# Low-rank gate of a two-layer decoder step: unrounded 32-bit products in quarters of the array in place of split products over its whole width

## The reference

```python
h = rms_norm(x, norm_g)                     # 2048 wide
proj = h @ w_in                             # c_lr is 16 of its columns
log_a = jax.nn.log_sigmoid((c_lr @ w_gate_lr + b_gate).astype(jnp.float32)) / C_GATE_TAU
o_c, new_S = gla_chunked(gq, gk, gv, log_a.reshape(bsz, L, C_HEADS, C_DK), gla_state)
```

## Time and profile before

| | us |
|---|---|
| median of three runs | 2256.7 |
| the profiled execution's own time | 2256.36 |
| its span, first to last instruction | 2254.6 |
| TensorE busy in it | 2247.4 (100% of the span) |
| VectorE busy | 1376.5 (61%) |
| ScalarE busy | 982.7 (44%) |

### The profile page before, as it was taken

The page is one execution under the profiler, slowest core; times in us unless marked ns, Lnnn a source line. Parts: engine busy times, 40 slices in busy tenths (PEclk is TensorE's granted clock), DMA queues, the critical chain, the costliest instruction groups (busy, mean ns, idle before and its releaser), DMA issues.

```text
span 2254.6 us, 40415 instructions
## 1 busy us (share of the span) xinstructions
PE 2247.4 (100%) x16664; PEld 2224.5 (99%) x16664; DVE 1376.5 (61%) x2453; ACT 982.7 (44%) x1788; POOL 77.6 (3%) x122
## 2 busy tenths in 40 slices
PE   9999999999999999999999999999999999999999
PEld 9999999999999999999999999999999999999999
DVE  6777767765545545446657777677645545545443
ACT  6454355644333333333344543556443333333332
POOL 1100100000000000000011001000000000000000
PEclk9999999999999999999999999999999999999999
DMA  7443654334444444445563437543344444444454
GB/s 287 150 160 132 233 195 141 129 126 150 150 150 150 150 150 150 150 150 196 191 220 134 161 129 247 192 149 112 130 149 151 150 150 150 151 150 151 149 197 150
DMA packets 100071, 364.12 MB, mean 162 GB/s; under 512 B 12288, under 2 KB 13056, under 8 KB 99056
## 3 DMA queue, kind: packets, MB, share of 16 engines
q1 hardware_dynamic: 88896, 317.76, 42.0%
q0 software_dynamic: 10128, 42.43, 5.3%
q10 hardware_dynamic: 864, 1.36, 0.2%
HBM read 341.65 MB, written 20.50 MB: 161 GB/s over the span
## 4 chain that ended last, share of the span: by engine, by line
PE 95%; DVE 2%; ACT 1%; issue 1%; DMA 0%; ACTq 0%; DVEq 0%
PE main L1693 90%; PE side L1693 4%; PE side L1697 1%; DVE w_lo L514 1%; ACT w_hi L1212 0%; DMA x_first<-in_x_pairs 0%; DVE sums L529 0%; PE side L1910 0%; PE side L1834 0%; DVE lev_e L778 0%; DVE ta L533 0%; PE side L1917 0%; DVE lev_q L529 0%; DVE lev_k L785 0%; DVE ext L600 0%
## 5 line engine op out<-in xcount | busy, mean ns | idle before, releaser
L514 DVE TENSOR_TENSOR w_lo<-raw,w_hi 128x512 fp32r<-128x512 f32 x1184 | 784.7, 697 | 493.4 <-ACT w_hi L1212 488.3
L1693 PE MATMUL main<-xg_hi,w_hi 128*128 128x320 f32 x3488 | 1084.4, 311 | 1.5 <-DVE w_lo L514 1.4
L1693 PE MATMUL main<-xg_lo,w_hi 128*128 128x320 f32 x3488 | 1077.2, 309 | 0.0
L1693 PE MATMUL main<-xg_hi,w_lo 128*128 128x320 f32 x3456 | 1067.9, 309 | 0.0
L1212 ACT ACTIVATE w_hi<-raw 128x512 fp32r<-128x512 f32 x1184 | 709.3, 626 | 695.2 <-PE main L1693 671.6
L1693 PEld LDWEIGHTS main<-xg_hi,w_hi 128*128 128x128 f32 x3488 | 654.8, 188 | 5.4 <-DVE xg_lo L548 1.5
L1693 PEld LDWEIGHTS main<-xg_lo,w_hi 128*128 128x128 f32 x3488 | 655.0, 188 | 0.2
L1693 PEld LDWEIGHTS main<-xg_hi,w_lo 128*128 128x128 f32 x3456 | 648.8, 188 | 0.0
L1693 PE MATMUL main<-branch_hi,w_hi 128*128 128x320 f32 x768 | 237.3, 309 | 0.0
L1693 PE MATMUL main<-branch_lo,w_hi 128*128 128x320 f32 x768 | 237.3, 309 | 0.0
L1693 PE MATMUL main<-branch_hi,w_lo 128*128 128x320 f32 x768 | 237.3, 309 | 0.0
(11 more groups left out here) (253 smaller groups left out, 1292.3 us busy)
## 6 DMA issues: line engine op xcount, KB each, us to landing
raw<-in_w_stream SPq DMA_DIRECT2D x595, 512.0 KB, 3.3
state<-in_state POOLq DMA_DIRECT2D x16, 512.0 KB, 4.8
out_state_s<-state POOLq DMA_DIRECT2D x16, 512.0 KB, 3.9
turned<-normed SPq DMA_DIRECT2D x40, 80.0 KB, 2.1
w_pool<-in_w_pool POOLq DMA_DIRECT2D x2, 1024.0 KB, 7.4
cache_k<-in_cache_k POOLq DMA_DIRECT2D x2, 1024.0 KB, 5.0
cache_v<-in_cache_v POOLq DMA_DIRECT2D x2, 1024.0 KB, 8.0
out_k_window<-in_cache_k_tok POOLq DMA_DIRECT2D x2, 960.0 KB, 10.3
```

The lines of the kernel that those rows point to most:

```text
L514: dve.tensor_tensor(w_lo[Q % RAWS][:, half], raw[Q % RAWS][:, half], w_hi[Q % HIS][:, half].bitcast(F32), ALU.subtract).then_inc(lo_ready, 1)
L1693: return pe.matmul(out, lhsT, rhs, start=start, stop=stop)
```

## The change

The blocks of the two low-rank beats are no longer rounded and split. DVE multiplies their 16 useful columns for each piece with the normalization gain into `w_rank` (`scale_rank`, one instruction for each of the two blocks). TensorE multiplies this with the plain x (`x_first`) as 32-bit floats, in four column quarters of the array: quarter q holds the 16 columns at 32 q and takes tokens 80 q to 80 q + 79. In layer 1 `x_first` is filled again from `y_mid` by eight loads of 320 KB, for which TensorE waits. The result lies in four row quarters; DVE reads it in four instructions of 16 x 80. The gate products run in four row quarters, 16 products of 16 rows with 128 columns and 80 tokens. The gate weights come in four loads for each layer, not eight. Since the two blocks need no `w_hi` buffer, the splits of blocks 10, 11 and 12 are put one or two beats earlier in the programs of ACT and DVE (`split_ahead`).

```diff
+def split_ahead(Q):
+    at = {LR_AT - 2: LR_AT + 2, LR_AT - 1: LR_AT + 2, LR_AT: LR_AT + 3, LR_AT + 1: LR_AT + 4}
+    return Q - Q % BEATS + at.get(Q % BEATS, Q % BEATS + 2)
...
+            def scale_rank(Q):
+                l, part = Q // BEATS, Q % BEATS - LR_AT
+                dve.wait_ge(raw_in[Q % RAWS], 16 * (Q // RAWS) + 16)
+                gain = par[:, l, R_NG + 8 * part:R_NG + 8 * part + 8].unsqueeze(2).to_broadcast([P, 8, RANK])
+                dve.tensor_tensor(w_rank[:, part, :].rearrange("p (k c) -> p k c", k=8),
+                                  raw[Q % RAWS][:, :].rearrange("p (k c) -> p k c", k=8)[:, :, 0:RANK], gain,
+                                  ALU.mult).then_inc(rank_ready, 1)
...
-                    dve.tensor_tensor(ta[:, 0, :], group_psum(GROUPS * l + LR_GROUP)[:, 0, :], rstd[:, :],
-                                      ALU.mult).then_inc(main_free, 1)
+                    low = group_psum(GROUPS * l + LR_GROUP)
+                    for q in range(4):
+                        rows, cols = slice(32 * q, 32 * q + RANK), slice(QUARTER * q, QUARTER * q + QUARTER)
+                        last = dve.tensor_tensor(ta[rows, 0, 0:QUARTER], low[rows, 0, 0:QUARTER], rstd[rows, cols],
+                                                 ALU.mult)
...
-                    split_lo_to(Q + 2)
+                    split_lo_to(split_ahead(Q))
...
-                    split_hi_to(Q + 2)
+                    split_hi_to(split_ahead(Q))
...
+                    for j in range(PAIRS):
+                        load(x_first[:, 2 * j:2 * j + 2, :], ins["y_mid"][j], x_again_in)
...
+            def rank_products(l, part, G):
+                bank = 2 * (G % 2)
+                pe.wait_ge(rank_ready, LR_BEATS * l + part + 1)
+                if l:
+                    pe.wait_ge(x_again_in, 16 * PAIRS)
+                for kk in range(8):
+                    k = 8 * part + kk
+                    for q in range(4):
+                        last = mm(main[32 * q:32 * q + RANK, bank, 0:QUARTER], w_rank[:, part, RANK * kk:RANK * kk + RANK],
+                                  x_first[:, k, QUARTER * q:QUARTER * q + QUARTER], k == 0, k == KT_D - 1)
+                    if kk % 4 == 3:
+                        last.then_inc(half_used, 1)
...
-                        rows = slice(2 * RANK * h, 2 * RANK * h + 2 * RANK)
-                        last = mm(side[:, h, 0:TOK], w_gate[rows, :], ta[rows, 0, :])
+                        for q in range(4):
+                            rows = slice(32 * q, 32 * q + RANK)
+                            last = mm(side[:, q, QUARTER * h:QUARTER * h + QUARTER], w_gate[rows, DK * h:DK * h + DK],
+                                      ta[rows, 0, 0:QUARTER])
```

More of the change, by code:

```diff
@@ L76, with is_rank, split_no, split_block @@
 LR_GROUP = LR_AT // 4
+QUARTER = TOK // 4
+def is_rank(Q):
+    return LR_AT <= Q % BEATS < LR_AT + LR_BEATS
+def split_no(Q):
+    l, beat = divmod(Q, BEATS)
+    return Q - LR_BEATS * (l + (beat >= LR_AT + LR_BEATS))
+def split_block(n):
+    l, i = divmod(n, BEATS - LR_BEATS)
+    return BEATS * l + i + (LR_BEATS if i >= LR_AT else 0)
+def split_ahead(Q):
+    at = {LR_AT - 2: LR_AT + 2, LR_AT - 1: LR_AT + 2, LR_AT: LR_AT + 3, LR_AT + 1: LR_AT + 4}
+    return Q - Q % BEATS + at.get(Q % BEATS, Q % BEATS + 2)
 C_COS, C_SIN, C_IDENT, C_BLOCK, C_KEEP, C_INVC, C_BSEL, C_END = 0, 320, 640, 768, 896, 1216, 1280, 1288
@@ L338, in trunk @@
         ones_r = place("ones_r", [P, P], F32R)
-        w_gate = place("w_gate", [P, DK], at=part_c + 12288 + 6144)
+        w_rank = place("w_rank", [P, LR_BEATS, 8 * RANK])
+        w_gate = place("w_gate", [P, GH * DK], at=part_c + 12288 + 6144)
         sq_hi = place("sq_hi", [P, 2, TOK], F32R, at=part_c + 8 * T1)
@@ L363, in trunk @@
         hi_ready = sem("hi_ready")
+        rank_ready = sem("rank_ready")
+        x_again_in = sem("x_again_in")
         lo_ready = sem("lo_ready")
@@ L469, in exchange @@
                             normed[32 * (q ^ 1):32 * (q ^ 1) + 32, :, :]).then_inc(swapped, 16)
[L471 to L479, removed]
         block = ctx.enter_context(nc.Block())
@@ L500, in split_lo_to @@
                 while lo_next[0] <= min(Q, BEATS * DEPTH - 1):
-                    split_lo(lo_next[0])
+                    (scale_rank if is_rank(lo_next[0]) else split_lo)(lo_next[0])
                     lo_next[0] += 1
@@ L507, in split_lo @@
                     half = slice(512 * s, 512 * s + 512)
[L508 to L513, removed]
-                    dve.tensor_tensor(w_lo[Q % RAWS][:, half], raw[Q % RAWS][:, half],
-                                      w_hi[Q % HIS][:, half].bitcast(F32), ALU.subtract).then_inc(lo_ready, 1)
+                    dve.wait_ge(hi_ready, split_no(Q) * 2 + (s + 1))
+                    dve.tensor_tensor(w_lo[Q % RAWS][:, half], raw[Q % RAWS][:, half],
+                                      w_hi[split_no(Q) % HIS][:, half].bitcast(F32), ALU.subtract).then_inc(lo_ready, 1)
+            def scale_rank(Q):
[5 more added lines that the diff above has]
+                                  ALU.mult).then_inc(rank_ready, 1)
             def wait_step(l, name, k):
@@ L679, in log_decay @@
                 for h in range(GH):
-                    v(dve.tensor_scalar(lev_q[:, h, :], side[:, h, 0:TOK], col(l, R_BG + h), None, ALU.add))
+                    v(dve.tensor_scalar(lev_q[:, h, :].rearrange("p (q t) -> p q t", q=4),
+                                        side[:, :, QUARTER * h:QUARTER * h + QUARTER], col(l, R_BG + h), None, ALU.add))
                 v.settle()
@@ L992, in vector_part @@
                     dve.wait_ge(half_used, last_half(l, beat))
-                    dve.tensor_tensor(ta[:, 0, :], group_psum(GROUPS * l + LR_GROUP)[:, 0, :], rstd[:, :],
-                                      ALU.mult).then_inc(main_free, 1)
+                    low = group_psum(GROUPS * l + LR_GROUP)
[3 more added lines that the diff above has]
+                                                 ALU.mult)
+                        if q < 3:
+                            v(last)
+                    last.then_inc(main_free, 1)
                     marks[("lr", l, 0)] = (main_free, GROUPS * l + LR_GROUP + 1)
@@ L1195, in split_hi_to @@
                 while hi_next[0] <= min(Q, BEATS * DEPTH - 1):
-                    split_hi(hi_next[0])
+                    if not is_rank(hi_next[0]):
+                        split_hi(hi_next[0])
                     hi_next[0] += 1
@@ L1206, in split_hi @@
                     if Q >= HIS:
[L1208 to L1212, removed]
+                        act.wait_ge(half_used, 2 * split_block(split_no(Q) - HIS) + s + 1)
+                    act.activation(w_hi[split_no(Q) % HIS][:, half], raw[Q % RAWS][:, half], ACT.Copy).then_inc(hi_ready, 1)
             def wait_step(l, name, k):
@@ L1548, in load_gate @@
             def load_gate(l):
[L1550 to L1553, removed]
+                for q in range(4):
+                    load(w_gate[32 * q:32 * q + RANK, :], ins["w_gate"][l], w_gate_in)
             load_gate(0)
@@ L1714, in block_products @@
                 for s in range(2):
-                    wh, wl = w_hi[Q % HIS], w_lo[Q % RAWS]
+                    wh, wl = w_hi[split_no(Q) % HIS], w_lo[Q % RAWS]
                     if opening is not None:
                         wait_mark(pe, "xg", opening, k0 // 2 + s)
-                    pe.wait_ge(lo_ready, Q * 2 + (s + 1))
+                    pe.wait_ge(lo_ready, split_no(Q) * 2 + (s + 1))
                     pairs = [(kk, t) for kk in range(2) for t in range(tiles)]
@@ L1740, in side_step @@
                     wm("rms_taken", l, 0)
-                    pe.wait_ge(w_gate_in, 128 * l + 128)
+                    pe.wait_ge(w_gate_in, 64 * l + 64)
                     for h in range(GH):
-                        rows = slice(2 * RANK * h, 2 * RANK * h + 2 * RANK)
-                        last = mm(side[:, h, 0:TOK], w_gate[rows, :], ta[rows, 0, :])
+                        for q in range(4):
+                            rows = slice(32 * q, 32 * q + RANK)
+                            last = mm(side[:, q, QUARTER * h:QUARTER * h + QUARTER], w_gate[rows, DK * h:DK * h + DK],
+                                      ta[rows, 0, 0:QUARTER])
                 elif name == "level":
@@ L1935, in _ @@
                             wait_main(G, G - 1)
-                        rank_products(Q, G, 8 * part, part == 0, part == 1)
+                        rank_products(l, part, G)
                     else:
```

## The result

The changed kernel takes 2262.68 us (median of ten runs, 2261.96 to 2266.23) against 2256.68 us before (ten runs, 2255.87 to 2258.55): ratio 1.0028, 95% interval 1.0020 to 1.0036. It is slower by 6.0 us. The forecast was 2258.6 us with a range up to 2262.0, so the prediction is wrong. What happened lies between its forecast and its third rival: block 10 landed later than forecast, but not as late as the rival had it, and a fall of the clock, which no rival had, came on top.

A forecast was written before the change was run, and what follows sets the result against it. Two tied chains, TensorE's and the gate's, were taken to bound the kernel and absorb the saving: 2256.36 + 0.5 (layer 0) + 1.7 (layer 1) = 2258.6 us, range 2254.3 to 2262.0.

The forecast's parts named there:

- third rival: Layer 1: window copies hold block 10 for 11.5 us, or x lands as late; +5.1, time 2262.0; chance 0.14.
- The low-rank products: Low-rank beats, each layer: 32 rounds of 70 ns, 2.57 us with switching against 4.70 before; TensorE saves 2.1 us.
- the 24 ns for each 16-column product: Low-rank products: 40 products in 0.96 us, taken to show the 60-cycle overhead is shared by quarters; 1.6 us left out.
- The gate products: Gate step, each layer: 1.25 us with switching against 0.95 before, 0.3 us slower (0 to 0.4).
- Layer 0: Layer 0: TensorE stands 0.7 us for cq, masks and lev_q start later, block 13 ready 0.5 us later: +0.5 us.
- the sign that was named: Layer 0: lev_q at 47.5 to 48.2 us, listed among the signs of a right prediction.
- Layer 1, the landing of block 10: Layer 1: block 10, issued at 1151.89, taken to land at 1160.0, nearest to block 9's row; +1.7 us.
- the prediction's own formula: Layer 1: loss is block 10's landing less 1158.3; time is 2256.36 + 0.5 + 1.7 = 2258.6 us.
- The clock: Layer 1: no clock term; after a 3.6 us stand, products 2.48, beat 10 3.52, gate step 1.25.
- x itself: Layer 1: x's loads, ahead of the copies, land about 1156 us; needed at 1159.3.
- The rule on the queues: Layer 1: no packet rule is written out; the third rival has the window copies hold block 10 11.5 us, chance 0.14.

The follow-up runs named there:

- late copies and the order near the old one: Changed kernel with the window copies moved into the mixing beats and only block 8 split ahead of cq at beat 6: 2253.82 us, ratio 0.9990.
- late masks: Changed kernel with window copies in the mixing beats, only block 8 split ahead of cq, and layer 0's masks at beat 16, not 10: 2253.14 us.
- the smaller pieces: Changed kernel with each window copy issued as four copies, bytes, place and order the same: 2263.36 us, ratio 1.0031.
- cq ahead: Changed kernel with DVE at beat 6 taking block 8, then reading cq, and blocks 9 and 10 at beat 7: 2260.40 us, ratio 1.0016.

## Why the prediction was wrong, step by step

**The low-rank products: right.** 2.57 us were forecast with the switching, and 2.41 is from the first record to the last one's end, which is another measure. In the chains the stretch from beat 5's end to the gate step took 15.26 us before and 13.10 us in the versions with late copies and the order near the old one, so 2.16 us saved where 2.13 were forecast. With waits away, the place from beat 5's end to beat 11 took 45.33 - 31.17 = 14.16 us (late masks) against 47.30 - 31.30 = 16.00 before: 1.84 us saved, products and gate together. The forecast was 2.13 - 0.3 = 1.83. One argument was weaker than it reads: the 24 ns for each 16-column product do not show that an overhead is shared by the quarters, as they would also come about if a product cost 24 ns at least. What the runs show is that nothing came on top: at 80 columns a product costs about 34 ns with the switching left out.

**The gate products: right.** 32 records last 1.13 us against 0.82 for 8, 0.3 us more, as forecast.

**Layer 0: mechanism right, size 0.5 off.** The wait for cq was 0.5 us (0.7 forecast), the four reads of 16 x 80 took 1.04 us, at the upper bound of my 0.5 to 1.1 (0.7 taken). But block 12 landed in 3.4 us in place of 4.1, which gave 0.7 back. The balance was zero, not +0.5: errors that cancelled. lev_q started at 48.30, which less the later first matmul (0.9 us) is 47.4, as before; the sign that was named, 47.5 to 48.2, did not show.

**Layer 1, the landing of block 10: the term that was mis-sized.** I took 8.1 us from issue to landing, nearest to block 9 before. It took 10.0 here and 10.1 to 11.45 in the four other profiles with the loads and the early copies. The rival had 11.5, from block 7. By the prediction's own formula 10.0 us give +3.6 in layer 1 and 2260.5 us in all: still inside the range. A reason is in the copies: I let them end 5.7 us later, at 1161; counted from the later start of that execution (0.95 us) this is 1162, and they ended at 1164.5. I had reckoned 2.62 MB at the mean rate of the busy stretch, 343 GB/s, 7.6 us, although that mean has the weight stream in it, while for x itself, in the same paragraph, I had taken the stream off. Measured from the issue of w_pool to the end of the last copy, the queue took 1155.5 - 1140.04 = 15.5 us before and 1164.5 - 1138.79 = 25.7 after: 10.2 us more for 2.62 MB, 256 GB/s. This lies between 343 and the 343 - 149 = 194 GB/s (13.5 us) that taking the stream off gives, as the engines had gaps before and moved 422 GB/s over the same stretch (1140 to 1158 us) after. The stream got 2.12 MB of that, 118 GB/s, where before it got 2.56 MB and TensorE uses 149 GB/s.

**The clock: a term left out, and the step that took the time out of the range.** The prediction let TensorE stand for 3.6 us in layer 1 and counted everything behind the stand (2.48 + 3.52 + 1.25) at full clock, without a reason. The stand was 5.2 us and brought TensorE to half clock for 6.8 us, worth 2.4 us in the profile and 1.3 to 1.5 in the medians. In the stands of 5.2, 6.6 and 4.3 us in layer 1 the clock fell; behind the one of 1.4 us it did not.

With both in its formula, layer 1 is (10.0 - 8.1) + 1.7 + 2.4 = 6.0; measured 5.9. The third rival's 2262.0 comes near the measured time, but by luck: it has a landing 1.5 us later than the one measured, and no clock.

**x itself: right.** No wait for its loads shows in any profile; the last of them landed at 1156.2, which less the later start of that execution is 1155.2 (about 1156 forecast).

**The rule on the queues.** By the Trainium skill (DMA: Bandwidth & Descriptors, Queues, rings and completion order) an engine switches between its queues only behind a whole packet, and a packet there is several descriptors. I had taken each piece of 61,440 bytes for such a packet, which the page does not state, let block 10 wait for at most two of them, and kept the third rival at 0.14 for it. In the trace GpSimd's queue moved 2.61 MB while block 10 waited, 163 KB for each of the 16 engines; two pieces are 123 KB, and the rest of the backlog stood in front too. How many descriptors went in one turn, no run here shows.

## What to carry to other kernels

An instruction that frees a buffer should not stand behind work for a later block in the same engine's program: its wait is then the later block's DMA. Loads added to a queue move everything behind them; price them at what full engines move less what the standing stream takes (an estimate here: 422 - 149 = 273 GB/s, 256 measured), not at the mean of a stretch, and look at which transfer the displaced ones now meet. Where TensorE would stand for several microseconds, add what the clock takes afterwards; and when two chains tie, a saving on one arrives only if each link of the other is moved too.

## What the runs showed of the hardware

- Products of 16 columns and 80 tokens in column quarters take about 70 ns for a round of four records, near 2 x 80 columns at 2.4 GHz (67 ns): 32 rounds in 2.41 us, with the 0.28 us of the last record in it.
- In a stand of 5.2 us the clock fell to 1.2 GHz 1.5 us before its end and stayed there for 6.8 us; with one of 6.6 us (the smaller pieces) it was 6.8 us too, with one of 4.3 us (cq ahead) 3.4 us. In the profile of the kernel with cq ahead, a stand of 2.9 us at the start of the run was followed by 3.4 us at half clock as well; stands of 2.4 and 2.3 us at the start of others were not.
- Matmuls of ones whose result nobody reads kept the clock at 2.4 GHz through the stand (1.00 in every stretch shown, against 0.50).
- While block 10 waited, the 16 DMA engines moved 409 GB/s, 2.61 MB for GpSimd's queue and 1.48 MB for the weight stream: a backlog on the one queue made a 512 KB load on the other take 10.0 us in place of 3.2 without it.
- Four DVE reads of 16 x 80 numbers took 1.04 us in layer 1 of the changed kernel, 0.26 each. Four of 128 x 320 (lev_q, with the masks late) took 1.93 us, 0.48 each: an eighth of the partitions and a quarter of the columns save only about half of the time (the two are not the same operation).
